# Modulation vectors of a two-block model: TensorE's column sums replaced by VectorE's running sums along each row

## The reference, cut to what matters

```python
silu_c, silu_cc = jax.nn.silu(c), jax.nn.silu(c_ctx)          # (1, 1024), (1024,)
for l in range(2):
    mod_x = (silu_c @ ada_w[l] + ada_b[l])[:, None, :]        # ada_w[l]: 1024 x 6144
    mod_c = silu_cc @ ada_w[l] + ada_b[l]
    # six vectors of 1024 each: shift, scale and gate of two sub-blocks, used as
    hx = rms_norm(x, norm_g[l, 0]) * (1 + sc1) + sh1          # ... x = x + g1 * rms_norm(y, ...)
```

## Time and profile before

| | us |
|---|---|
| median of 3 runs (2303.3 to 2304.95) | 2303.89 |
| the profiled execution | 2299.75 |
| its span, first to last instruction | 2297.9 |
| TensorE matmul busy | 2194.2 (95%) |
| VectorE busy | 1605.1 (70%) |
| ScalarE busy | 1041.6 (45%) |
| GpSimd busy | 210.4 (9%) |

### The profile page before, as it was taken

One profiled execution on the slowest core, in us unless ns is written; L12 is line 12 of the kernel. 1 busy time (PEld: TensorE's weight loads), 2 busy tenths in 40 slices (PEclk: granted clock), 3 DMA queues, 4 the chain that ended last, 5 costly groups with the idle time before them and its releaser, 6 DMA issues. The chain is left out here.

```text
span 2297.9 us, 35725 instructions
## 1 busy us (share of the span) xinstructions
PE 2194.2 (95%) x15008; PEld 2007.0 (87%) x15008; DVE 1605.1 (70%) x2406; ACT 1041.6 (45%) x1513; POOL 210.4 (9%) x219
## 2 busy tenths in 40 slices
PE   6999998999999999899999998999999997997997
PEld 6999978999999997899998776798888886587997
DVE  5878896978887887797852467576445337757775
ACT  5433534433544353544443345535444324755662
POOL 2100232100210032210000001000000000100000
PEclk9999999999999998999998999999999998998999
DMA  5665524667466552476622121023222222113553
GB/s 211 238 224 202 195 74 178 235 221 257 185 228 222 194 184 74 184 275 226 216 87 75 38 73 62 20 74 111 92 102 100 92 75 91 37 46 115 184 175 106
DMA packets 47487, 331.75 MB, mean 144 GB/s; under 512 B 5532, under 2 KB 6652, under 8 KB 8288
## 3 DMA queue, kind: packets, MB, share of 16 engines
q1 hardware_dynamic: 37808, 266.35, 32.8%
q0 software_dynamic: 9520, 63.11, 7.1%
HBM read 328.40 MB, written 1.05 MB: 143 GB/s over the span
## 5 line engine op out<-in xcount | busy, mean ns | idle before, releaser
L2005 DVE TENSOR_TENSOR WLO<-RAW,WHI 128x2048 fp32r<-128x2048 f32 x252 | 583.6, 2317 | 257.7 <-ACT WHI L1453 254.7
L459 PE MATMUL PS<-XB,WHI 128*128 128x256 f32 (+1 forms) x3072 | 701.5, 324 | 16.7 <-DVE XB L2353 12.4
L1453 ACT CAST WHI<-RAW 128x2048 fp32r<-128x2048 f32 x252 | 476.1, 1892 | 312.3 <-DMA RAW<-in_dn_c 78.1
L459 PEld LDWEIGHTS PS<-XB,WHI 128*128 128x128 f32 x3072 | 518.0, 192 | 63.6 <-issue 19.1
L459 PE MATMUL PS<-XHI,WHI 128*128 128x272 f32 (+1 forms) x1760 | 513.4, 294 | 18.7 <-ACT XHI L1461 15.1
L459 PE MATMUL PS<-XHI,WLO 128*128 128x272 f32 (+1 forms) x1760 | 508.2, 291 | 0.0
L459 PE MATMUL PS<-XB,WLO 128*128 128x256 f32 (+1 forms) x1536 | 494.2, 322 | 0.0
L459 PE MATMUL PS<-XLO,WHI 128*128 128x272 f32 (+1 forms) x1760 | 486.1, 290 | 0.0
L459 PEld LDWEIGHTS PS<-XHI,WHI 128*128 128x128 f32 x1760 | 339.5, 193 | 24.2 <-issue 18.9
L459 PEld LDWEIGHTS PS<-XHI,WLO 128*128 128x128 f32 x1760 | 339.1, 193 | 0.0
L459 PEld LDWEIGHTS PS<-XLO,WHI 128*128 128x128 f32 x1760 | 328.2, 192 | 0.4
(11 more groups left out here) (363 smaller groups left out, 2713.2 us busy)
## 6 DMA issues: line engine op xcount, KB each, us to landing
AW<-in_ada POOLq DMA_DIRECT2D x48, 1024.0 KB, 7.2
RAW<-in_up_c SPq DMA_DIRECT2D x44, 1024.0 KB, 4.9
RAW<-in_up_a SPq DMA_DIRECT2D x42, 1024.0 KB, 4.9
RAW<-in_up_b SPq DMA_DIRECT2D x42, 1024.0 KB, 4.9
RAW<-in_mix SPq DMA_DIRECT2D x30, 1024.0 KB, 4.9
RAW<-in_dn_a SPq DMA_DIRECT2D x22, 1024.0 KB, 4.9
RAW<-in_dn_b SPq DMA_DIRECT2D x22, 1024.0 KB, 4.9
RAW<-in_dn_c SPq DMA_DIRECT2D x22, 1024.0 KB, 4.9
```

The costliest lines, as they stand in the source:

```text
L459: return pe.matmul(o, w, x, start=first, stop=last)
L1453: act.copy(WHI1[:, s, 0:w], RAW[:, s, 0:w]).then_inc(w1_high, 1)
L2005: v.tensor_tensor(WLO1[:, s, 0:w], RAW[:, s, 0:w], WHI1[:, s, 0:w].bitcast(F32), ALU.subtract)\
```

## The change

The weights lie transposed on the host: a partition holds one output feature, and its 1024 input features run along the row. The two conditioning vectors come broadcast to all partitions (`SCB`, 1 MB), are put through Silu on ScalarE as a 128x2048 operation, and each VectorE instruction multiplies a row of 1024 weights by a vector and gives its sum straight into `MODF`. A piece of 1 MB holds 2 tiles of 128 outputs, so 4 instructions. `ada_reduce`, `ada_take`, `ada_done` and `ada_taken` go. The mixer overwrites SCB's place, so it is loaded three times (start, and behind each mixer), and Silu is done three times, in feed-forwards 0, 1 and 3.

```diff
@@ gpsimd
-            for dst, name in ((PL[:, :, :], "x"), (LNIN[:, :, :], "ln_in"), (SC[:, :, :], "c")):
+            for dst, name in ((PL[:, :, :], "x"), (LNIN[:, :, :], "ln_in")):
...
+            def condition_load():
+                pool.dma_start(SCB[:, :, :], A["c"]).then_inc(cond_loaded, 16)
+
+            condition_load()
             for h in range(ADA_RING):
                 ada_load(h)
...
             def mixer(l):
-                pool.wait_ge(ada_done, 6 * (2 * l + 1))
+                pool.wait_ge(ada_step, ADA_OPS * (2 * l + 1))
...
                     if h == 2:
                         pool.wait_ge(tile_out, 8 * q + 8)
+                        condition_load()
                     ada_load(12 * (2 * l + 1) + h)
@@ instructions of each step
             def ada_due(step):
             if step < FT:
-                return 0 if step == FT - 1 else 2 if step in (11, 15, 19) else 3
-            return 4 if step < FT + DN_EARLY else 0
+                return 0 if step in (0, FT - 1) else 1 + step % 2
+            return 2 if step < FT + DN_EARLY else 0
@@ tensor: up steps, down steps, behind the norm's statistics
-                    if f in (8, 13, 19):
-                        n = (8, 13, 19).index(f)
-                        ada_reduce(6 * i + n, 0, 4 * i + n)
...
-                            if k == 0 and j == 7:
-                                pe.wait_ge(ada_taken, 4 * i + 3)
...
-                for n in range(3, 6):
-                    ada_reduce(6 * i + n, 8 * (n - 3), 4 * i + 3)
@@ scalar
+            def condition(n):
+                act.wait_ge(cond_loaded, 16 * (n + 1))
+                act.activation(SCB[:, :, :], SCB[:, :, :], ACT.Silu).then_inc(silu_c, 1)
...
                 silu(0)
                 silu(1)
+                if i != 2:
+                    condition((i + 1) // 2)
                 gate_high(0)
@@ vector
             def gains(l):
-                v.wait_ge(ada_taken, 8 * (l + 1))
+                v.wait_ge(ada_step, 2 * ADA_OPS * (l + 1))
+                m = MODF[:, 48 * l:48 * l + 48, :]
+                v.tensor_tensor(m, m, ADAB[:, 48 * l:48 * l + 48].rearrange("p (a o) -> p a o", o=1)
+                                .to_broadcast([P, 48, 2]), ALU.add).then_inc(mod_biased, 1)
+                v.wait_ge(mod_biased, l + 1)
...
             def ada_ops(i, step):
+                    if n % ADA_OPS == 0:
+                        v.wait_ge(silu_c, (i + 1) // 2 + 1)
+                    if n >= 2:
                         v.wait_ge(ada_step, n - 1)
-                        v.scalar_tensor_tensor(a, w, c, a, ALU.mult, ALU.add).then_inc(ada_step, 1)
+                    w = AW[:, h % ADA_RING, t % 2, :]
+                    v.scalar_tensor_tensor(PROD[:, :] if g == 0 else w, w, 1.0, SCB[:, g, :], ALU.mult, ALU.mult,
+                                           accum_out=MODF[:, t, g:g + 1]).then_inc(ada_step, 1)
```

More of the change, by code:

```diff
@@ L40 @@
 NEG = -1e30
-N_X, N_START = 3, 2
+N_X, N_START = 2, 2
 N_SET = 9
@@ L103, in build @@
         ONES = small.put("ONES", [3, P])
-        SC = small.put("SC", [CT, 2])
         ADAB = small.put("ADAB", [DEPTH * 48])
@@ L170, in build @@
         adab = Row("B")
-        AW = adab.put("AW", [ADA_RING, 4, 512])
-        AP_ = adab.put("AP", [ADA_RING, 2, 512])
+        AW = adab.put("AW", [ADA_RING, 2, D])
+        SCB = adab.put("SCB", [2, D])
+        PROD = adab.put("PROD", [D])
         XB = place("B", "XB", 0, [2, 2, CT, SEQ], F32R)
@@ L318, in build @@
         ada_loaded = [sem(f"ada_loaded{s}") for s in range(ADA_RING)]
-        ada_step, ada_done, ada_taken = sem("ada_step"), sem("ada_done"), sem("ada_taken")
+        ada_step, cond_loaded, mod_biased = sem("ada_step"), sem("cond_loaded"), sem("mod_biased")
         in_mean, in_centred, in_squared, in_var = sem("in_mean"), sem("in_centred"), sem("in_squared"), sem("in_var")
@@ L423, in unit_of @@
             return l * UNITS_LAYER + (0, UNITS_MIX0, UNITS_B0)[stage] + n
+        ADA_OPS = 48
         def ada_due(step):
             if step < FT:
[L429 to L430 removed]
+                return 0 if step in (0, FT - 1) else 1 + step % 2
+            return 2 if step < FT + DN_EARLY else 0
         ADA_FROM = [0]
         for n in range(FFN_STEPS):
[L434 to L435 removed]
+            ADA_FROM.append(min(ADA_FROM[-1] + ada_due(n), ADA_OPS))
+        assert ADA_FROM[-1] == ADA_OPS, ADA_FROM
         class Steps:
@@ L511, in ada_load @@
                 if h >= ADA_RING:
-                    pool.wait_ge(ada_step, 8 * (h - ADA_RING + 1))
-                pool.dma_start(AW[:, h % ADA_RING, :, :], A["ada"][h, :, :].rearrange("p (k c) -> p k c", k=4))\
+                    pool.wait_ge(ada_step, 4 * (h - ADA_RING + 1))
+                pool.dma_start(AW[:, h % ADA_RING, :, :], A["ada"][h, :, :].rearrange("p (t c) -> p t c", t=2))\
                     .then_inc(ada_loaded[h % ADA_RING], 16)
+            def condition_load():
+                pool.dma_start(SCB[:, :, :], A["c"]).then_inc(cond_loaded, 16)
+            condition_load()
             for h in range(ADA_RING):
@@ L561, in ffn @@
                     for h in range(ADA_RING, 12):
-                        if ADA_FROM[step] < 8 * (h - ADA_RING + 1) <= ADA_FROM[step + 1]:
+                        if ADA_FROM[step] < 4 * (h - ADA_RING + 1) <= ADA_FROM[step + 1]:
                             ada_load(12 * i + h)
@@ L619, in _ @@
                     pool.dma_start(VEC[:, :], A["vec"][l + 1, :, :]).then_inc(vec_loaded, 16)
-            pool.wait_ge(ada_done, 24)
+            pool.wait_ge(ada_step, 4 * ADA_OPS)
+            pool.wait_ge(tile_out, 8 * 6)
             for dst, name in ((IDN[:, :], "ident"), (FCW[0][:, :, :, :], "fcw0"), (FCW[1][:, :, :, :], "fcw1"),
@@ L738, in mean_half @@
                 last.then_inc(half_mean, 1)
[L740 to L749, removed]
             def norm_stats(q, sl):
@@ L2023, in ada_ops @@
             def ada_ops(i, step):
-                for n in range(96 * i + ADA_FROM[step], 96 * i + ADA_FROM[step + 1]):
-                    b, k, g, h = n // 16, n % 16 // 2, n % 2, n // 8
-                    if n % 8 == 0:
+                for n in range(ADA_OPS * i + ADA_FROM[step], ADA_OPS * i + ADA_FROM[step + 1]):
+                    t, g, h = n // 2, n % 2, n // 4
+                    if n % 4 == 0:
                         v.wait_ge(ada_loaded[h % ADA_RING], 16 * (h // ADA_RING + 1))
[L2029 to L2034, removed]
-                        v.wait_ge(ada_step, n - 1)
-                        v.scalar_tensor_tensor(a, w, c, a, ALU.mult, ALU.add).then_inc(ada_step, 1)
[L2038 to L2044, removed]
+                    if n % ADA_OPS == 0:
+                        v.wait_ge(silu_c, (i + 1) // 2 + 1)
+                    if n >= 2:
+                        v.wait_ge(ada_step, n - 1)
+                    w = AW[:, h % ADA_RING, t % 2, :]
+                    v.scalar_tensor_tensor(PROD[:, :] if g == 0 else w, w, 1.0, SCB[:, g, :], ALU.mult, ALU.mult,
+                                           accum_out=MODF[:, t, g:g + 1]).then_inc(ada_step, 1)
             def pair(c, tk):
@@ L2183, in ffn1 @@
                 norm(q)
-                ada_take(6 * i + 3, 3, 6 * i + 6)
             def mixer(l):
@@ L2745, in ada_halves @@
 def ada_halves(w):
-    return w.reshape(2, 4, P, 12, 512).transpose(3, 0, 2, 1, 4).reshape(24, P, 2 * D)
+    return w.T.reshape(24, 2, P, D).transpose(0, 2, 1, 3).reshape(24, P, 2 * D)
 def shape_tables():
@@ L2801, in lay_out @@
     a["ctx"] = feature_major(i["ctx_2"][0])
-    a["c"] = columns(np.stack([i["c_ctx_2"], i["c_2"][0]])).transpose(0, 2, 1)
+    a["c"] = np.broadcast_to(np.stack([i["c_ctx_2"], i["c_2"][0]]), (P, 2, D))
     a["ln_in"] = columns(np.stack([i["ln_in_g"], i["ln_in_b"]]))
```

13 lines of the change are left out of this document (1 added, 12 removed).

## The result

The changed kernel takes 2280.75 us (median of 4 runs, 2276.64 to 2285.12) against 2303.94: ratio 0.9899, 95% interval 0.9876 to 0.9923. 23 us or 1.0% faster; 2282.2 had been predicted. Its profiled execution took 2284.02 us, span 2282.2, 15.7 us less than the 2297.9 before.

A forecast was written before the change was run, and what follows sets the result against it. TensorE was taken to bound the up steps, busy 117.00 of 117.00 us, with VectorE having slack. Terms 20.4 + 1.0 + 1.1 - 0 - 1.0 - 0.3 + 0.5 gave 21.7 us less, a median of 2282.2 us, range 2278 to 2291.

The forecast's parts named there:

- (a): Feed-forward up steps: 12 reductions of 1.70 us each leave TensorE's path, 20.4 us less.
- (b): First down unit of each feed-forward: tile 7's wait of 0.3 us goes, about 1 us less in all four.
- rival B: Smaller gain: feed-forward starts and VectorE's slack give back 2 to 3 us per feed-forward, 2292 us; chance 0.23.
- (c): Norm gap behind feed-forward 0: without reductions TensorE starts 1.1 us earlier; nothing gained in the other gaps.
- (d): TensorE's clock behind three norm gaps that now stand idle: no difference, bounds -3 to +3 us.
- (e): Way into the second block: statistics may run at low clock behind a new gap; 1 us lost, bounds 0 and 2.
- (f): VectorE's 1024-column product with sum: 1.4 us each, bounds 1.2 and 2.3, covered by TensorE, 0 us on the path.
- Rival A: Slower: the running sum halves VectorE's rate, about 2.4 us an instruction, 2364 us; chance 0.08.
- (g): Starts of feed-forwards 0, 1, 3: VectorE waits for SCB's Silu after T, end of TensorE's first two units; 0.3 us lost.
- (h): DMA and GpSimd's queue: three added 1 MB loads of SCB arrive before they are needed, cost 0.
- (i): Start of the kernel: the load TensorE's first product waits for is issued one place earlier; gain 0.5 us, bounds 0 and 1.
- (j): Bias: two VectorE additions of 96 columns replace 16 small ones beside TensorE's work, 0 us.

The follow-up runs named there:

- experiments 2: Changed kernel with eight unused one-column matmuls put back where each up-step reduction stood; 2298.23 us, 0.9959 to the kernel before.
- experiment 3: Kernel before with each reduction's eight one-column matmuls made one of eight columns, sums over g and j left out; 2282.61 us, ratio 0.9893.
- experiment 1: The changed kernel timed and profiled again with no edit; 2281.81 us, 0.9885 to the kernel before.
- experiment 5: Changed kernel with VectorE's last gate product, gate(21), moved ahead of the rest of unit 23; 2276.6 us, 0.9869 to the kernel before.
- experiment 10: Changed kernel with 24 unused one-column matmuls behind each feed-forward's norm statistics, filling the norm gaps; 2280.16 us, 0.9886 to the kernel before.
- experiment 9: Changed kernel with each row product over 512 of its 1024 columns, loads unchanged; 2277.95 us, 0.9869 to the kernel before.
- experiment 4: Changed kernel with each of its 192 row products done twice on VectorE, the first without a sum; 2406.0 us, 1.0433 to the kernel before.

## Why the prediction was right

The forecast's mechanism held: experiments 2 and 3 show the gain to be TensorE's time in the up steps. Its sum of 21.7 stands against 23.2 by medians and against 20.0 and 20.7 by the stages outside the mixers; that it lies so near the median is in part luck, since some 3 us of that are in no stage, and since what (a) and (b) gave was cut by losses that no term had. Step by step, by the prediction's letters:

- (a) Right in kind, 1.79 us for a reduction instead of 1.70: 21.5 for 20.4. The earlier trace rows was read from start to start of one; the silus' pitch has it better.
- (b) Tile 7's own wait is gone: no pitch of TensorE stands out there. With (a) it came out as 17.4 to 19.1 us in the feed-forwards instead of 21.4. What is missing was rival B's kind of loss, but not where B put it: four waits for gate(21), 4.0 us (two, 2.9 us, in experiment 1), because a reduction behind unit 19 was cover for a gate queued behind a remainder that waits for its weights; and 1.2 us in feed-forward 1 in both profiles, where ScalarE waited 8.2 and 6.4 us for a late load of weights and TensorE, no longer held up by reductions, for WLO. Nothing in the text looked behind the last up step. With that order changed (experiment 5) the feed-forwards give 24.1.
- (c) Right: 8.47 to 7.40 us, 1.07 for 1.1, in all profiles with idle gaps. Behind feed-forwards 1 and 2 0.0 and 0.1.
- (d) Right within the spread: behind the first gap the granted clock was 0.53 and 0.82 with idle gaps and 0.57 with a filled one (experiment 10).
- (e) Inside its bounds: the stretch from statistics to the first product of the second block is 0.6 us longer, where 1.0 was taken, but 0.2 in experiment 1 and nothing in most of the others.
- (f) 1.15 us, where 1.4 was taken and 1.2 was the lower bound: the row with 746 ns at 512 columns gave 1276, the chip 1219, and the reading of the sum is hidden. This error cost nothing, since nearly all of it was covered (experiment 9). The point from which VectorE decides was wrong in the other direction. I worked it out from steps of 272 columns and took no collisions in; in feed-forward 3 it is 1.83 and not 2.07, and with 1.9 us an instruction the gain is already zero. (The prediction's own formula gives 22 us at 2.12, not 2.15.) Rival A, priced 82 us over the forecast at 2.4 us, measures 124 at 2.52; it had VectorE's time and left out that TensorE's clock falls behind the waits, some 42 us.
- (g) gate(0) begins at 46.08, T (41.1) plus 5.0, and TensorE waits for nothing from 41 to 75 us: 0 for 0.3.
- (h) Right; the load of SCB lands 11.2 to 14.4 us after its issue, some 10 us or more before its Silu.
- (i) TensorE's first instruction comes at 12.04 us instead of 12.71, 0.7 for 0.5. The first unit starts 1.6 us earlier in the profile after, but only 0.2 earlier in experiment 1 (28.22 against 28.40), so the spread of the start is larger than the gain.
- (j) Right, 0.255 us each.

Left out altogether were the mixers: each moves by 4 to 5 us between the two profiles of the changed kernel, more than all steps but (a), and together they are 9.7 of the 10.8 us between these. That the other runs' times differ by the mixers too is likely, but they have no profile.

## What to carry to other kernels

Matmuls of one column in the list of a bound TensorE cost 0.22 us each; eight of them came down to 0.22 us in all as one matmul of eight columns, where the sums allow that (here they don't: experiment 3 leaves sums out); else they belong to an engine with slack. Whoever takes work off the bound engine should look at each place where the next engine's queue holds a waiting instruction in front of a needed one: the removed work was its cover, and a change of order there gave another 4 to 6 us on 23. An engine that is made to wait can lose more than the wait: a third of experiment 4's 124 us was TensorE's lower clock. Slack is to be worked out in the tightest stage, here the feed-forward with 256 columns, and with collisions.

## What the runs showed of the hardware that was not expected

- VectorE's sum along a row costs next to no time beside its product: 1225 ns against 1219 without it for 1024 columns (experiment 4), 1.15 us from one to the next, with an 83 ns reading that overlaps the next one.
- VectorE's instructions with two inputs in SBUF and GpSimd's exclude each other for whole instructions, in two patterns: in turns (a tap every 0.93 to 1.5 us instead of 0.41), or GpSimd shut out for as long as VectorE's list lasts (four operations 10.19 us instead of 3.65, three 13.90 instead of 5.89). What picks the pattern stays open.
- TensorE's clock can fall to its lower level in the middle of dense work: for 13 us behind a wait of 2.56 us (0.50 from 319 to 332 us), but also for 5 us without such a wait (experiment 1). Mixers with the wait are longer than the same mixer without it by 3.3 to 6.3 us (mixer 0) and 2.5 to 5.7 (mixer 1), the wait included.
- A reduction's matmuls cost by the instruction: 0.22 us with one column and with eight (experiments 2 and 3).
